# Moving mixer pieces between weight blocks of a two-layer hybrid decoder kernel

## The reference

```python
h = x + 0.5 * swiglu(rms_norm(x, ffn1_norm), ffn1_w_in, ffn1_w_out)
u = rms_norm(h, mix_norm)
proj = u @ w_in          # inputs of the four branches, and 4 x 1024 gate channels
y_sb  = stick_breaking_attention(sb_q, sb_k, sb_v)
y_s5  = s5_mixer(s5_u, ...)       # diagonal complex state space; y = states @ C + d * u
                                  # gelu(y) @ w_glu, split in ga, gb: ga * sigmoid(gb)
y_gla = gla_mixer(gq, gk, gv, gr, gg, ...)   # chunked gated linear attention
y_dsa = dilated_mixer(d_q, d_k, d_v, ...)    # dilated sliding-window softmax attention
per_branch = einsum('bsnw,nwd->bsnd', [y_sb, y_s5, y_gla, y_dsa], w_branch)
mixed = sum_n(sigmoid(gates) * per_branch)
h = h + mixed @ w_out
h = h + 0.5 * swiglu(rms_norm(h, ffn2_norm), ffn2_w_in, ffn2_w_out)
```

## Time and profile before

| | us |
|---|---|
| median of 3 runs | 1227.83 |
| the profiled execution | 1229.41 |
| its span, first to last instruction | 1227.4 |
| PE busy | 1215.5 |
| DVE busy | 928.7 |
| ACT busy | 682.6 |
| GpSimd (POOL) busy | 349.6 |

### The profile page before, as it was taken

The page is one execution under the profiler, slowest core; times in us unless marked ns, Lnnn a source line. Parts: engine busy times, 40 slices in busy tenths (PEclk is TensorE's granted clock), DMA queues, the critical chain, the costliest instruction groups (busy, mean ns, idle before and its releaser), DMA issues.

```text
span 1227.4 us, 23522 instructions
## 1 busy us (share of the span) xinstructions
PE 1215.5 (99%) x9146; PEld 1144.4 (93%) x9146; DVE 928.7 (76%) x1170; ACT 682.6 (56%) x1025; POOL 349.6 (28%) x496
## 2 busy tenths in 40 slices
PE   9999999999999999999999999999999999999998
PEld 8999989998999999999999999999989999999998
DVE  6867788897687876666786778788986787766665
ACT  5666646673553564545566655557636445554553
POOL 0088991440304200000001889906203041000000
PEclk9999999999999999999999999999999999999999
DMA  8654454443344565455445454554433446545441
GB/s 309 242 205 160 182 178 169 168 172 111 131 172 172 206 248 205 172 179 197 172 171 207 171 205 171 175 199 141 171 115 128 172 173 239 205 172 203 168 176 69
DMA packets 32322, 220.36 MB, mean 180 GB/s; under 512 B 3712, under 2 KB 4352, under 8 KB 6272
## 3 DMA queue, kind: packets, MB, share of 16 engines
q1 hardware_dynamic: 31824, 218.91, 49.8%
q10 hardware_dynamic: 432, 0.52, 0.1%
HBM read 218.37 MB, written 1.05 MB: 179 GB/s over the span
## 4 chain that ended last, share of the span: by engine, by line
PE 92%; DVE 4%; ACT 2%; issue 1%; DMA 1%; SPq 0%; ACTq 0%
PE banks L567 22%; PE banks L522 19%; PE banks L523 18%; PE banks L524 18%; PE banks L569 11%; PE banks L535 4%; DVE w_lo_t L1282 2%; DMA hT<-x_t 1%; ACT w_hi_t L946 0%; ACT attB L1196 0%; ACT attB L1194 0%; DVE dqk L1703 0%; ACT attB L1221 0%; ACT L1202 0%; DVE dqk L1705 0%
## 5 line engine op out<-in xcount | busy, mean ns | idle before, releaser
L1282 DVE TENSOR_TENSOR w_lo_t<-raw,w_hi_t 128x1024 fp32r<-128x1024 f32 x394 | 494.9, 1296 | 99.8 <-ACT w_hi_t L946 99.4
L946 ACT ACTIVATE w_hi_t<-raw 128x1024 fp32r<-128x1024 f32 x394 | 393.5, 1046 | 128.6 <-PE banks L524 124.3
L522 PE MATMUL banks<-u_t,w_hi_t 128*128 128x256 f32 x928 | 265.9, 286 | 4.3 <-DVE G L1811 3.1
L523 PE MATMUL banks<-u_t,w_hi_t 128*128 128x256 f32 x928 | 262.8, 283 | 0.0
L524 PE MATMUL banks<-u_t,w_lo_t 128*128 128x256 f32 x928 | 262.7, 283 | 0.0
L567 PE MATMUL banks<-b_t,w_hi_t 128*128 128x512 f32 x576 | 204.0, 398 | 0.0
L567 PE MATMUL banks<-u_t,w_hi_t 128*128 128x512 f32 x576 | 204.0, 398 | 0.0
L522 PE MATMUL banks<-h_hi_t,w_hi_t 128*128 128x256 f32 x672 | 190.2, 283 | 0.0
L523 PE MATMUL banks<-h_lo_t,w_hi_t 128*128 128x256 f32 x672 | 190.1, 283 | 0.0
L524 PE MATMUL banks<-h_hi_t,w_lo_t 128*128 128x256 f32 x672 | 190.1, 283 | 0.0
L522 PEld LDWEIGHTS banks<-u_t,w_hi_t 128*128 128x128 f32 x928 | 178.3, 192 | 9.3 <-issue 4.0
(11 more groups left out here) (273 smaller groups left out, 1980.8 us busy)
## 6 DMA issues: line engine op xcount, KB each, us to landing
raw<-weights SPq DMA_DIRECT2D x201, 1024.0 KB, 4.8
raw<-weights SPq DMA_DIRECT2D x3, 512.0 KB, 8.7
prm<-params SPq DMA_DIRECT2D x1, 1250.5 KB, 5.4
prm<-params SPq DMA_DIRECT2D x1, 1238.5 KB, 10.0
raw<-weights SPq DMA_DIRECT2D x4, 256.0 KB, 6.9
out_t<-hT SPq DMA_DIRECT2D x4, 256.0 KB, 2.2
cst<-constants SPq DMA_DIRECT2D x1, 704.0 KB, 10.0
hT<-x_t SPq DMA_DIRECT2D x1, 512.0 KB, 7.4
```

Source lines behind the costliest of these rows:

```text
L522: pe.matmul(o, st[0], mv[0], start=start, stop=False, skip_group_check=True)
L523: pe.matmul(o, st[0], mv[1], start=False, stop=False, skip_group_check=True)
L946: act.activation(w_hi[:, slot, a:a + HALF], raw[:, slot, a:a + HALF], ACT.Copy) \
L1282: dve.tensor_tensor(w_lo[:, slot, a:a + HALF], raw[:, slot, a:a + HALF], w_hi[:, slot, a:a + HALF].bitcast(F32), ALU.subtract) \
```

## The change

`S5_OUT` moves: the first state outputs from entry 11 to 13, the second from 17 to 19. The dilated output and the GLU matmuls move from entry 20 to 21 on PE, and what follows them on ACT and DVE moves by one entry as well: the output `y` from 20 to 21, the three `branch_lo` from 21 to 22. The inner GELU becomes a function, and DVE calls it in entry 19 ahead of `evacuate(19)`, no longer in entry 17. Tanh moves from 18 to 19 and the GELU product from 19 to 20. `s5_turn(2)` moves from the end of entry 12 to the end of entry 11. The norm sums (`SS_AFTER`) of norm 0 and norm 1 go one part later in the first two blocks, and the row of norm 1 (`ROW_AFTER`) goes behind the last part. Layer 0's norm 0 has code of its own and keeps its place.

```diff
-SS_AFTER, ROW_AFTER = (4, 4, 4), 6
+SS_AFTER, ROW_AFTER = (5, 5, 4), 7
-S5_OUT = {11: 0, 17: 1}
+S5_OUT = {13: 0, 19: 1}
...
-                        if m == 20:
+                        if m == 21:
                             pe.wait_ge(s.s5_inner, layer * PER.s5_inner + 1)
...
-                    if m == 18:
+                    if m == 19:
                         act.wait_ge(s.s5_inner, layer * PER.s5_inner + 1)
...
-                    if m == 20:
+                    if m == 21:
                         act.wait_ge(s.y, layer * PER.y + 1)
...
+                def gelu_inner():
+                    root = math.sqrt(2 / math.pi)
+                    dve.wait_ge(s.s5_y, layer * PER.s5_y + 2)
...
                                                    ALU.mult))
+                        s5_turn(2)
                     if m == 12:
...
-                    if m == 17:
-                        dve.wait_ge(s.s5_y, layer * PER.s5_y + 2)
...
-                    if m == 19:
+                    if m == 20:
                         dve.wait_ge(s.s5_tanh, layer * PER.s5_tanh + 1)
...
-                    if m == 20:
+                    if m == 21:
                         dve.wait_ge(s.s5_sig, layer * PER.s5_sig + 1)
...
-                    if m == 21:
+                    if m == 22:
                         branch_lo(2, 1, yb[:, 1, :, :].rearrange("p a t -> p (a t)"), 0.5)
                         branch_lo(3, 2, banks[:, 3, :], 1.0)
                         branch_lo(1, 3, yb[:, 0, :, :].rearrange("p a t -> p (a t)"), 0.25)
...
-                    if m == 12:
-                        s5_turn(2)
...
                                 dve.tensor_copy(attB[:, h, :], banks[:, DSA_BANK[h], 0:ATT]).then_inc(s.dsa_pte_v, 1)
+                            gelu_inner()
                         if not BY_ACT[m]:
                             evacuate(m)
```

More of the change, by code:

```diff
@@ L1630, in gla_mask @@
                                              in1=causal, op0=ALU.min, op1=ALU.mult).then_inc(s.gla_attm, 1)
+                def gelu_inner():
+                    root = math.sqrt(2 / math.pi)
+                    dve.wait_ge(s.s5_y, layer * PER.s5_y + 2)
+                    for k in range(2):
+                        n = own.mark(dve.scalar_tensor_tensor(
+                            out=s5g[:, 0, k * T:(k + 1) * T], in0=s5u[:, k, :], scalar=p_("s5_d")[:, k:k + 1],
+                            in1=banks[:, 3, k * T:(k + 1) * T], op0=ALU.mult, op1=ALU.add))
+                    own.wait(n)
+                    own.link(dve.tensor_tensor(s5g[:, 1, :], s5g[:, 0, :], s5g[:, 0, :], ALU.mult))
+                    own.link(dve.tensor_scalar(s5g[:, 1, :], s5g[:, 1, :], 0.044715 * root, root,
+                                               ALU.mult, ALU.add))
+                    dve.tensor_tensor(s5g[:, 1, :], s5g[:, 1, :], s5g[:, 0, :], ALU.mult) \
+                        .then_inc(s.s5_inner, 1)
                 def pieces(m):
```

## The result

The changed kernel takes 1242.84 us (median of 4 runs, 1241.52 to 1246.73) against 1228.49 us for the kernel before (4 runs, 1227.65 to 1229.19), a ratio of 1.0124 with a 95% interval of 1.0102 to 1.0147. The forecast was 1239.9 us, in a range of 1236 to 1244, slower with a chance of 0.95. The profiled execution took 1241.82 us against 1229.41, 12.4 us more, and its span is 1239.7 us.

What follows compares the result with a forecast made beforehand. PE, busy 99% of the span, was taken to bound the kernel. Two layers' 10.4 us, less 0.5 for norms, gave +9.9; with +2.2 for the clock, on the median of 1227.83, 1239.9 us, range 1236 to 1244.

Steps and rivals of the forecast that it cites:

- The hole at out0: Before `out0`, PE waits for DVE's three `branch_lo`, now behind the evacuation that waits for block 22: +5.5 us per layer.
- The GELU product: At the GLU matmuls, PE waits for DVE's late GELU product: +2.5 us per layer.
- the walk: Step-by-step clock of PE and DVE from entry 17 to `out0`, in layer 0's trace: +6.4 us at `out0`.
- Entry 19's evacuation: Before block 21, PE waits for this DVE evacuation, now behind the inner GELU: +0.4 us per layer.
- The holes that close: PE's waits at the transposes behind entry 14 (1.24 us) and at block 20 (1.57 us) go, per layer.
- The joined group: `s5_out(1)` joins the transposes, saving the way in and out of a small group on PE: -0.2 us per layer.
- The norms: Norm sums and norm 1's row moved later, so PE waits less for the squares: -0.5 us for the kernel.
- The clock: Slow clock behind the two `out0` holes of 5.5 us, 1.1 us each: +2.2 us.
- The bound of 1.7 per hole: Upper bound of the clock loss behind each long hole: half of the 3.4 us slow stretch in layer 0's trace.
- the clock stays up: Rival: no clock loss through the holes, +9.9 us, 1237.7 us; chance 0.22.
- falls behind every long hole: Rival: the clock falls behind all four long holes, 1.7 us each, 1244.5 us; chance 0.15.
- The rival in which the kernel is faster: Block 22's end stays covered and the GELU product comes before `attend` ends: -6.5 us, 1221.3 us; chance 0.03.

Runs made afterwards that it cites:

- b_lo22: The kernel before with one edit, the three `branch_lo` in entry 22 instead of 21: 1243.66 us, ratio 1.0115.
- lo21: The changed kernel with the three `branch_lo` back in entry 21, everything else as changed: 1229.48 us, ratio 1.0009.
- lo21_prod19: The changed kernel with `branch_lo` in entry 21 and the GELU product in entry 19, ahead of the GLA norm's root: 1221.43 us, ratio 0.9942.
- b_turn11: The kernel before with `s5_turn(2)` alone moved to the end of entry 11: 1226.72 us, ratio 0.9987.
- lo22_first: The changed kernel with `branch_lo` still in entry 22, but ahead of the remainder of block 25: 1236.38 us, ratio 1.0065.

## Why the prediction was right, point by point

- *The hole at out0, +5.5 per layer.* Right: 5.45, and the same edit alone gives the same hole and the same total time (b_lo22), while undoing it takes both away (lo21).
- *The GELU product, +2.5.* Right: 2.38. As in the walk, DVE waited once, 0.49 us for ACT's rounding ahead of the remainder of block 21, and then had no idle time up to the product. Moving the product away (lo21_prod19) against lo21 brings 6.6 us by the profiled executions (1227.96 and 1221.36) where 4.8 were reckoned; the slow stretch behind entry 11 that lo21 had, 1.5 us, fills most of the rest. The medians are 8.0 us apart; the last 1.5 of those go with the clock, which averaged 0.997 in most executions of lo21 and 1.000 in most of lo21_prod19.
- *Entry 19's evacuation, +0.4.* Right: 0.41.
- *The holes that close, 1.24 and 1.57.* Right: neither is left in the changed kernel.
- *The joined group, -0.2.* Right: from 334.68 to 337.20 PE spends 2.52 - 0.12 = 2.40 us on it. The two groups before took 1.09 and 342.67 - 339.51 - 1.57 - 0.12 = 1.47, together 2.56.
- *The norms, -0.5.* Small, but mis-sized: about -0.9. The wait for the evacuation of `s5u`, expected at some 0.5, is 0.24 us per layer.
- *The clock, +2.2, is the term that failed in size.* "I take 1.1 behind each of the two holes of 5.5, less than 1.7 since part of the slow stretch falls into the hole." Part of it does, but the slow stretch was twice as long as the 3.4 us of the earlier trace rows. In layer 0, (1 - 0.77) x 5.6 / 0.5 = 2.6 us of it lie in the hole and 4.1 + 0.2 on work behind it, 6.9 in all; in layer 1, 2.0 and 4.8. It cost 1.9 and 2.2 us, 4.1 in all. The bound of 1.7 per hole, taken from the one stretch of 3.4 us, was too low behind a hole of 5.5; for that stretch itself it was a little high, since the same kind of stretch costs 1.5 us by PE's starts (lo21). The rule of the Trainium skill ("TensorE: Matmul & The Clock Gate", on the HAM clock gate), that an idle array falls back to half rate, agrees with the 0.50 behind both holes.

Per layer these terms are -1.24 - 1.57 - 0.16 + 0.41 + 2.38 + 5.45 = 5.3. The terms as the prediction lists them add to 5.4, and it took 5.2 by its walk. Twice 5.3, with 4.1 for the clock and -0.9 for the norms, is 13.8 us. The profiled executions differ by 12.4. The slow stretch behind entry 11 of layer 0, which the changed kernel did not have in its profiled execution, explains the gap: from its start, 282.02, to the small matmuls behind the second block that follows, 296.27, PE takes 14.25 us, and 294.72 - 282.01 = 12.71 in b_turn11, where the clock is up, so it cost 1.5 us. The walk's times are 3 us later than the trace's (371.6 against 368.43 for `out0`), as it left out what changes ahead of entry 17.

The rivals "the clock stays up" and "falls behind every long hole" are both out for the profiled execution: it fell behind the holes at `out0`, not behind the GLU's. The other executions of the changed kernel, of which no trace was taken, have clocks of 0.990 to 0.994 and reach 1246.73 us, so more slow stretches than these two occur. The rival in which the kernel is faster named the right lever: with the holes mended it measured 1221.4 us where 1221.3 was worked out. That the two agree to 0.1 us is in part luck, since the rival left out the 0.41 us per layer for entry 19's evacuation and took the norms 0.4 too small.

What stays open is what makes the clock fall behind 2.63 us in one place and not behind 2.38 in another, and behind entry 11's small matmuls in some of the profiled executions only.

## What to carry to other kernels

Ask of every step that is moved past another on an in-order engine what the step now ahead of it waits for: three short instructions of 1.9 us put behind a wait for PE's own latest block turned a slack of 0.2 us into 5.5 us of mutual waiting per layer. Judge the pieces of a change one by one: here four moves were worth 6 to 7 us together, and one placed too late by a single entry cost twice that. A hole in the engine that bounds the kernel costs its length and can cost the clock behind it (1.6 us behind one of 2.63, 1.9 to 2.2 behind one of 5.45), so price both from the start. And where single slow stretches come and go between executions, compare executions of like granted clock before reading a difference of 1 or 2 us.

## What the runs showed of the hardware

- Behind a hole of 5.45 us TensorE's granted clock was 0.50 (1.2 GHz) for 4.1 and 4.7 us of work. Behind one of 2.63 us it stood at 1.00 through the hole and averaged 0.57 and 0.60 over the next 4 us. Through the GLU's hole of 2.38 us it stayed at 1.00 in the traces of the changed kernel, lo22_first and lo21. I had thought 2.5 us too short for a fall.
- The clock also fell with no hole ahead of it. Behind entry 11's dense small matmuls it was at half speed in the kernel before (layer 0), in lo21 and in b_turn11 (layer 1), and in neither layer of lo21_prod19, whose mean granted clock is 1.00. Each such stretch cost 1.5 us. In the kernel before, two groups of executions lie about that far apart: 1227.4 to 1227.9 us at a clock of 1.000, 1228.8 to 1229.5 at 0.998 to 0.999.
- At half clock a matmul of 256 columns starts every 0.21 us in `out0`, at full clock every 0.12.
